# Mix order, y by token halves and v prepared ahead in the gate stage of a decoder trunk

## The reference, cut to what matters

```python
z = gelu(rms_norm(x, g_norm) @ w_in)
u, v = split(z, 2, axis=-1)
v = rms_norm(v, g_v).reshape(b, nc, CHUNK, 8, 128)
sv = einsum("gts,bnsgc->bntgc", tril(w_s), v) + b_s   # mixes the tokens of a chunk, for each of 8 groups g
y = u.reshape(b, nc, CHUNK, 8, 128) * sv
x = x + y.reshape(b, s, 1024) @ w_out
```

## Time and profile before

| what | value |
|---|---|
| median of 3 runs (lowest to highest) | 2029.73 us (2027.12 to 2032.08) |
| the profiled execution, own time | 2034.66 us |
| its span, first to last instruction | 2032.9 us |
| TensorE busy, share of the span | 96% |
| VectorE, ScalarE, GpSimd busy | 74%, 46%, 22% |
| mean granted TensorE clock | 0.98 of full speed |

### The profile page before, as it was taken

One profiled execution on the slowest core, in us unless ns is written; L12 is line 12 of the kernel. 1 busy time (PEld: TensorE's weight loads), 2 busy tenths in 40 slices (PEclk: granted clock), 3 DMA queues, 4 the chain that ended last, 5 costly groups with the idle time before them and its releaser, 6 DMA issues.

```text
span 2032.9 us, 27966 instructions
## 1 busy us (share of the span) xinstructions
PE 1947.5 (96%) x9704; PEld 1649.4 (81%) x9704; DVE 1503.0 (74%) x2202; ACT 933.9 (46%) x1620; POOL 445.5 (22%) x321
## 2 busy tenths in 40 slices
PE   7999899999999998999999799989999999989999
PEld 7988778788888886888999688867788888867887
DVE  5356658888888875786844688889887887866875
ACT  5233434544444443444412788756444444433443
POOL 0000001333333220020110445532333333310100
PEclk9999999999999998999999799999999999999999
DMA  4111142122222259680112000011222222289761
GB/s 170 43 42 42 52 155 104 62 83 83 83 82 83 83 174 311 192 207 1 42 42 69 15 11 12 22 78 68 84 83 83 83 83 83 83 240 339 142 143 63
DMA packets 62820, 198.99 MB, mean 98 GB/s; under 512 B 5008, under 2 KB 5136, under 8 KB 55568
## 3 DMA queue, kind: packets, MB, share of 16 engines
q1 hardware_dynamic: 48080, 163.29, 22.6%
q0 software_dynamic: 14656, 34.61, 7.9%
HBM read 162.22 MB, written 35.65 MB: 97 GB/s over the span
## 4 chain that ended last, share of the span: by engine, by line
PE 80%; DVE 10%; DMA 4%; ACT 3%; issue 1%; SPq 0%; POOL 0%; DVEq 0%; ACTq 0%
PE banks L2082 26%; PE banks L2084 26%; PE banks L2083 26%; DMA raw<-in_w_f_out 1%; DMA b<-c_scratch 1%; DVE t_lo L1600 1%; DMA c_scratch<-xT 1%; ACT lg L1302 1%; PE banks L2418 1%; DVE t_sum L1840 1%; DVE t_sum L1590 1%; DVE lg L1982 1%; DVE small L1989 1%; DVE fw_lo L1756 1%; DVE xT L1682 1%
## 5 line engine op out<-in xcount | busy, mean ns | idle before, releaser
L2082 PE MATMUL banks<-t_hi,fw_hi 128*128 128x512 f32 x1248 | 488.8, 392 | 11.0 <-issue 11.0
L2084 PE MATMUL banks<-t_hi,fw_lo 128*128 128x512 f32 x1248 | 486.9, 390 | 0.0
L2083 PE MATMUL banks<-t_lo,fw_hi 128*128 128x512 f32 x1216 | 474.6, 390 | 0.0
L2082 PEld LDWEIGHTS banks<-t_hi,fw_hi 128*128 128x128 f32 x1248 | 235.5, 189 | 61.3 <-issue 12.6
L2084 PEld LDWEIGHTS banks<-t_hi,fw_lo 128*128 128x128 f32 x1248 | 235.2, 188 | 49.3
L2083 PEld LDWEIGHTS banks<-t_lo,fw_hi 128*128 128x128 f32 x1216 | 229.4, 189 | 48.1 <-issue 0.5
L2082 PE MATMUL banks<-fw_hi,fw_hi 128*128 128x512 f32 x544 | 215.6, 396 | 22.4 <-DVE fw_lo L1756 22.4
L667 POOL TENSOR_TENSOR nrm<-raw 128x512 f32<-128x512 f32 x40 | 53.6, 1339 | 753.7 <-DVE fw_lo L1643 439.7
L2083 PE MATMUL banks<-fw_lo,fw_hi 128*128 128x512 f32 x544 | 214.4, 394 | 0.0
L2084 PE MATMUL banks<-fw_hi,fw_lo 128*128 128x512 f32 x544 | 214.4, 394 | 0.0
L1133 ACT ACTIVATE fw_hi<-b 128x512 fp32r<-128x512 f32 x154 | 96.9, 630 | 220.8 <-PE banks L2084 209.4
(11 more groups left out here) (196 smaller groups left out, 4208.5 us busy)
## 6 DMA issues: line engine op xcount, KB each, us to landing
raw<-in_w_f_in SPq DMA_DIRECT2D x44, 1024.0 KB, 4.9
c_scratch<-xT SPq DMA_DIRECT2D x44, 512.0 KB, 2.6
raw<-in_w_f_out SPq DMA_DIRECT2D x66, 256.0 KB, 6.6
b<-c_scratch SPq DMA_DIRECT2D x16, 1024.0 KB, 9.0
a_sum<-in_w_f_out POOLq DMA_DIRECT2D x16, 1024.0 KB, 10.4
w_raw<-in_w_ao SPq DMA_DIRECT2D x16, 512.0 KB, 3.5
x_scratch<-xT SPq DMA_DIRECT2D x4, 2048.0 KB, 7.2
xT<-x_scratch SPq DMA_DIRECT2D x8, 1024.0 KB, 9.4
```

The lines of the kernel that those rows point to most:

```text
L2082: nc.tensor.matmul(out, w_h, m_h, start=start, stop=False, **kw)
L2083: nc.tensor.matmul(out, w_h, m_l, start=False, stop=False, **kw)
L2084: return nc.tensor.matmul(out, w_l, m_h, start=False, stop=stop, **kw)
```

## The change

TensorE: mix 0 now stands between the two token halves of u tile 1, and mix 7 between those of tile 7; a new semaphore, `u_half`, tells that the first half of tile 7 is through. The other mixes stay between the tiles. The y of token half 0 is made into operands from that moment; the y of half 1 is made beside projection tiles 0 to 3. Projection tile 0 runs seven k steps before tile 1 begins. v is scaled one group further ahead (`normalised(g + 2)` behind `mixed(g)`), and the two parts of the next vn are made before mixed(g) and not after it. The diff, without the renamed semaphore and the loops' headers:

```diff
 # GpSimd: y_done starts at 1
+            pool.sem_inc(y_done, 1)
 # ScalarE
             def mixed(g):
                 act.wait_ge(mix_full, g_n.add())
+                act.wait_ge(y_done, g_n.now())
...
             def u_step(g, s):
+                act.wait_ge(mix_full, g_n.now(1))
+                vn_upper(g_n.now(2))
                 mixed(g)
-                vn_upper(g_n.now(1))
                 gate(1 - s)
...
+            act.wait_ge(mix_full, 7)
+            vn_upper(8)
             mixed(6)
-            vn_upper(8)
-            def y_upper(g):
-                act.wait_ge(y_done, g + 1)
-                nc.scalar.activation(h_hi_a[:, bass.ds(g, 1), :].rearrange("p a (n t) -> p (a n) t", t=P),
-                                     v_sb[:, :, bass.ds(g * P, P)], ACT.Copy).then_inc(y_hi_done, 1)
+            def y_upper(half, g):
+                tok, n = slice(half * HALF, (half + 1) * HALF), slice(4 * half, 4 * half + 4)
+                act.wait_ge(y_done, g + 2)
+                nc.scalar.activation(h_hi_a[:, g, tok].rearrange("p (n t) -> p n t", t=P),
+                                     v_sb[:, n, g * P:(g + 1) * P], ACT.Copy).then_inc(y_hi_done, 1)
+            act.wait_ge(u_half, 1)
+            for g in range(5):
+                y_upper(0, g)
+            mixed(7)
+            for g in (5, 6):
+                y_upper(0, g)
             act.wait_ge(tile_full[1], tiles[1].add())
-            y_upper(0)
-            y_upper(1)
             split(1)
-            mixed(7)
             act.wait_ge(u_scaled[1], tiles[1].now())
             nc.scalar.activation(ug[:, 1, :], ug[:, 1, :], ACT.Gelu).then_inc(tile_free[1], 1)
-            with act.Fori(2, KT) as g:
-                y_upper(g)
+            y_upper(0, 7)
...
+            for dt in range(KT):
+                o_square(dt // 2, dt % 2, 0)
+                split(dt % 2)
+                if dt < 4:
+                    for g in (2 * dt, 2 * dt + 1):
+                        y_upper(1, g)
 # VectorE (y_lower by halves in the same manner)
             def u_step(g, s):
+                vn_lower(g_n.now(2))
                 mixed(g, s)
-                normalised(g + 1, g_n.now(1))
+                normalised(g + 2)
                 tiles[1 - s].add()
                 scaled_u(1 - s)
                 split(1 - s)
...
+            vn_lower(8)
             mixed(6, 0)
-            normalised(7, 8)
-            tiles[1].add()
-            scaled_u(1)
-            y_lower(0)
-            y_lower(1)
-            split(1)
-            mixed(7, 1, lambda: y_lower(2))
-            with dve.Fori(3, KT) as g:
-                y_lower(g)
+            def last_tile():
+                for g in (5, 6):
+                    y_lower(0, g)
+                tiles[1].add()
+                scaled_u(1)
+                split(1)
+            for g in range(5):
+                y_lower(0, g)
+            mixed(7, 1, last_tile)    # runs it behind the bias, before the product with u
+            y_lower(0, 7)
...
+            for dt in range(KT):
+                o_add(dt // 2, dt % 2, 0)
+                split(dt % 2)
+                if dt < 4:
+                    for g in (2 * dt, 2 * dt + 1):
+                        y_lower(1, g)
 # TensorE
+            def rows_around(slot, s, between, signal=None):
+                pe.wait_ge(w_ready[slot], use[slot].add())
+                if tiles[s].some():
+                    pe.wait_ge(tile_free[s], tiles[s].now())
+                rows_half(slot, s, 0, h_hi_a, h_lo_a, signal)
+                between()
+                rows_half(slot, s, 1, h_hi_a, h_lo_a)
             rows(0, 0, h_hi_a, h_lo_a)
-            mix(0)
-            rows(1, 1, h_hi_a, h_lo_a)
+            rows_around(1, 1, lambda: mix(0))
...
-            mix(7)
+            mix(5)
+            rows(0, 0, h_hi_a, h_lo_a)
+            mix(6)
+            rows_around(1, 1, lambda: mix(7), u_half)
             pe.wait_ge(mix_free, KT)
...
-            for k in (0, 1):
+            for k in range(KT - 1):
                 pe.wait_ge(y_ready, k + 1)
                 o_step(0, 0, k)
             pe.wait_ge(w_ready[1], use[1].now())
-            for k in (0, 1):
+            for k in range(4):
                 o_step(1, 0, k)
-            for k in range(2, KT):
-                pe.wait_ge(y_ready, k + 1)
-                for s in range(2):
-                    o_step(s, 0, k)
+            pe.wait_ge(y_ready, KT)
+            o_step(0, 0, KT - 1)
+            for k in range(4, KT):
+                o_step(1, 0, k)
...
-            o_tile(0, 1)
+            o_tile(0, 1, True)    # waits for the y of half 1 at each k
```

More of the change, by code:

```diff
@@ L373, in build @@
         mix_free = sem("mix_free")
-        ug_done = sem("ug_done")
+        u_half = sem("u_half")
         y_done = sem("y_done")
@@ L979, in o_square @@
                                      .rearrange("p a t -> p (a t)"), ACT.Square).then_inc(sq_done, 1)
-            def o_body(i):
-                for s in range(2):
-                    o_square(i, s, 0)
-                    split(s)
             nc.scalar.preload_act_table(ACT.Sqrt)
-            loop(0, 4, [(use[0], 1), (use[1], 1)], o_body)
+            for dt in range(KT):
[4 more added lines that the diff above has]
+                        y_upper(1, g)
             for dt in range(KT):
@@ L1508, in _, with normalised @@
             dve.wait_ge(bs_landed, 16)
-            def normalised(g, n):
-                vf = nrm[:, 0, :].rearrange("p (n c) -> p n c", c=P)
+            vf = nrm[:, 0, :].rearrange("p (n c) -> p n c", c=P)
+            def normalised(g):
                 nc.vector.tensor_tensor(vf, v_sb[:, :, bass.ds(g * P, P)],
@@ L1515, in normalised, with vn_lower @@
                                         ALU.mult).then_inc(vf_done, 1)
+            def vn_lower(n):
                 dve.wait_ge(vn_hi_done, n)
@@ L1528, in mixed @@
                 dve.wait_ge(mix_free, g_n.now())
+                link(nc.vector.tensor_tensor(m, m, bs_bc[:, bass.ds(g, 1), :].broadcast_to([P, NCH, P]), ALU.add))
                 between()
-                link(nc.vector.tensor_tensor(m, m, bs_bc[:, bass.ds(g, 1), :].broadcast_to([P, NCH, P]), ALU.add))
                 dve.wait_ge(tile_free[s], tiles[s].now())
@@ L1543, in _ @@
             dve.wait_ge(rows_kept, 2)
-            normalised(0, 1)
+            normalised(0)
+            vn_lower(1)
             scaled_u(0)
             split(0)
+            dve.wait_ge(vn_ready, 1)
+            normalised(1)
             def u_step(g, s):
+                vn_lower(g_n.now(2))
                 mixed(g, s)
-                normalised(g + 1, g_n.now(1))
+                normalised(g + 2)
                 tiles[1 - s].add()
@@ L1558, in _, with y_lower @@
             loop(0, 3, [(use[0], 1), (use[1], 1), (g_n, 2), (steps, 2), (tiles[0], 1), (tiles[1], 1)], u_body)
+            vn_lower(8)
             mixed(6, 0)
-            normalised(7, 8)
-            tiles[1].add()
-            scaled_u(1)
[L1564 to L1569, removed]
-            y_lower(0)
-            y_lower(1)
-            split(1)
-            mixed(7, 1, lambda: y_lower(2))
-            with dve.Fori(3, KT) as g:
-                y_lower(g)
+            def y_lower(half, g):
+                tok, n = slice(half * HALF, (half + 1) * HALF), slice(4 * half, 4 * half + 4)
+                dve.wait_ge(y_hi_done, KT * half + g + 1)
+                nc.vector.tensor_tensor(h_lo_a[:, g, tok].rearrange("p (n t) -> p n t", t=P),
+                                        v_sb[:, n, g * P:(g + 1) * P],
+                                        h_hi_a[:, g, tok].rearrange("p (n t) -> p n t", t=P).bitcast(F32),
+                                        ALU.subtract).then_inc(y_ready, 1)
+            def last_tile():
[8 more added lines that the diff above has]
+            y_lower(0, 7)
             link(nc.vector.memset(acc[:, :, :], 0.0))
@@ L2127, in rows, with rows_half @@
                     pe.wait_ge(tile_free[s], tiles[s].now())
[L2128 to L2135, removed]
+                rows_half(slot, s, 0, h_hi, h_lo)
+                rows_half(slot, s, 1, h_hi, h_lo)
+            def rows_half(slot, s, half, h_hi, h_lo, signal=None):
+                tok = slice(half * HALF, (half + 1) * HALF)
+                for k in range(KT):
+                    mm = three(banks[:, 2 * s + half, :], w_hi[:, slot, k * P:(k + 1) * P],
+                               w_lo[:, slot, k * P:(k + 1) * P], h_hi[:, k, tok], h_lo[:, k, tok],
+                               k == 0, k == KT - 1)
+                if half:
+                    mm.then_inc(tile_full[s], 1)
+                    tiles[s].add()
+                elif signal is not None:
+                    mm.then_inc(signal, 1)
+            def rows_around(slot, s, between, signal=None):
[5 more added lines that the diff above has]
+                rows_half(slot, s, 1, h_hi_a, h_lo_a)
             outs = [Count() for _ in range(2)]
```

(11 more changed lines are left out.)

## The result

The changed kernel takes 2017.87 us (median of 5 runs, 2014.76 to 2019.81) against 2029.73 (5 runs, the 3 of the table above and two more, 2027.12 to 2032.08). The ratio is 0.9935, 95% interval 0.9923 to 0.9947, which is 13.2 us less, 10.8 to 15.6. The forecast was 2014.4 in a range of 2009.5 to 2020.5, faster.

The account below looks back on a forecast made before the run. TensorE, busy 1947.5 of 2032.9 us, was taken as the bound, so only its idle or low clock could pay. Gains of 5.9 + 5.7 + 2.0 + 1.7 = 15.3 us gave a median of 2014.4, range 2009.5 to 2020.5.

Parts of the forecast that it names:

- Gap A: TensorE's 3.10 us idle before mix 0; moving mix 0 inside u tile 1 was to gain 5.9 us, clock included.
- gap B: TensorE's idle between mix 7 and the output projection, 4.00 us; claimed to vanish, gaining 5.7 us, clock included.
- gap C: TensorE's idle before projection tile 2, awaiting weights; claimed 1.40 in place of 3.44 us, gaining 2.0, plus 1.7 of clock.
- The clock term: Slow clock behind the three idles, claimed regained: 1.7 in mix 0, 1.1 in tile 1, 1.5 and 1.7 in projection tiles.
- Cost zero: Preparing the next v ahead on ScalarE and VectorE: same number of instructions, claimed to cost zero, its 4.0 us chain covered.
- The prediction's other sum, 13.5: Split of y: if a half cost a whole, piece 7 would miss by about 2, gain 13.5 us, not 15.4.
- (1): Whole kernel as summed: 2014.4 us, own range 2011.5 to 2017.5, chance 0.70.
- (2): Remaining idle before projection tile 2 halves the clock or exceeds 2 us: 1.7 to 3.5 less gain, 2016 to 2018, chance 0.10.
- (3): Last y(7) or slot 1's split is late, idle returns before piece 7: gain only 9.6, 2020 us, chance 0.12.
- (4): Slower: every mix waits for the vn and gain chain of 4.0 us, costing 28 against 15.3, 2042 us, chance 0.02.
- (5): The gain is given back at a later wait that doesn't move with TensorE: 2029.7 us, chance 0.03.
- (6): No idle at all before projection tile 2: 2013 us, chance 0.03.

Follow-up runs that it names:

- before: The kernel before, unchanged, in its first profiled execution; that execution took 2034.66 us, against a median of 2029.73.
- same_again: The kernel before, unchanged, timed and profiled again; 2029.92 us beside 2030.91, ratio 0.9996.
- ahead_only: The kernel before with only v prepared ahead (loops over y and projection tiles of half 0 written out); 2031.7 us, ratio 0.9998.
- the timed filler: The kernel before with matmuls of no use filling the three idle gaps of the stage; 2029.31 us beside 2032.06, ratio 0.999.
- no_ahead: The changed kernel with v prepared as before, behind mixed(g), both mixes still inside their tiles; 2029.62 us, ratio 0.9991 to the kernel before.
- head_only: The kernel before with only mix 0 moved between the token halves of u tile 1; 2033.75 us, ratio 1.0013.
- whole_y: The changed kernel with y made whole after tile 7 and projection tiles 0 and 1 interleaved; 2026.32 us, ratio 0.9976 to the kernel before.
- after: The changed kernel in its first profile, span 2013.0 us; median 2017.87 us, ratio 0.9935 to the kernel before.
- after_again: The changed kernel, unchanged, timed and profiled again; 2016.55 us beside 2031.24 for the kernel before, ratio 0.9935.
- no_head: The changed kernel with mix 0 back between u tiles 0 and 1; 2022.49 us, ratio 0.9956 to the kernel before.
- order_2: The changed kernel with projection tile 0's last k step behind 2, not 4, steps of tile 1; 2016.22 us, ratio 0.9929 to the kernel before.

## Why the prediction was right, and where it was off

**The idle, right to a few tenths.** Gap A gone, gap B gone, gap C from 3.44 to 1.17 where I had 1.40 (the step is 1.40, of which one matmul's 0.23 is work), full clock in tile 2, steps of 12.82 in the middle: each is in the timeline after. Slacks were 2.0 and 2.1 where I had 1.1 and 1.3, because I added up instructions at their full length and in a row they overlap: five half-size ones take 3.09, not 3.45, and whole-size ones of 1.22 start 1.13 to 1.21 apart. Tile 3's weights, priced as tight, came 0.9 early, and no tenths were lost.

**The clock term, mis-sized as an average.** The sum took 6.0 us of slow clock (1.7, 1.1, 1.5, 1.7) out of one execution, and took it off the median, though this execution stood 4.9 us over the median. Three profiles with all three gaps of the kernel before have S = 135.64, 132.49 and 132.10 (before, same_again, ahead_only), mean 133.4; the changed kernel has 120.21 twice. The gain in S is thus 15.4, 12.3 and 11.9, on average 13.2. That both ratios say 13.2 as well is in part luck, with three draws. At clock 1.00 S is 130.80, so the low clock costs 2.6 on average by these three and 1.7 by the timed filler, not 6.0. That puts the forecast of 2014.4 some 2 us too fast (medians 2017.87 and 2016.55), though 15.3 lies within the intervals of both timings, so that the times alone don't refute it.

**"Cost zero" of preparing v ahead, right as a cost and wrong as a reading.** My chain of 4.0 us against 5.45 and 10.9 was for the new order. I didn't work out what the old order would need, 8.9 us after a mix where the new one needs 2.8, and so didn't see that both moved mixes hang on this part. no_ahead shows it for both and head_only for mix 1: without it the gaps come back in front of mix 1 and mix 7 and the whole change is worth 0 to 3.5 us. The total came out right because the change has both parts.

**The split of y.** Its 16 instructions are busy for 10.2 us on VectorE against 9.4 for the 8 whole ones; the rule of the Trainium skill against many small tiles (VectorE: DVE Perf Modes, "The TRN2 errata") holds in direction, with under 1 us, and all of it lies beside TensorE. In return whole_y, which gives up the halves and the step order together, is 9.0 to 9.8 us slower. The prediction's other sum, 13.5 if a half cost a whole, counted five halves only; with seven in front of piece 7, and its own two, the same working makes it some 3.4 late, not 2 (an estimate). No half cost that much.

**Rivals.** The first median, 2017.87, lies just outside the own range of (1), 2011.5 to 2017.5, and inside that of (2); the second, 2016.55, lies in both. So the time doesn't choose between them, the traces do. (2), a low clock behind the rest of gap C: not drawn in after, after_again, no_head or no_ahead, all with a step of 1.40. (3), a late last chain: no. (4), the chain as a wait in every step: no, the middle steps are 12.82 as before. (5), given back later: no sign. From projection tile 3 to the end of the span it is 1784.6 and 1785.1 us in the two profiles of the changed kernel, and 1787.5, 1786.2 and 1787.3 in before, same_again and ahead_only. (6), no gap C: not in this kernel, but one number away (order_2).

## What to carry to other kernels

A gap in front of a small step isn't closed by moving the step: work out how long after its predecessor the step's operands are ready, for the old order of the feeding engines too; the reordering that seems to cost and gain nothing may be what the others hang on. Low clock behind an idle has to be taken from several traces. Idle itself repeated to hundredths in this stage, so one trace was enough there; it doesn't everywhere (the 1.57 at 1814.21 in the earlier trace rows is 1.15 in same_again). Where two projection tiles share a feed, finish one of them early enough for the chain of its next weights.

## What the runs showed of the hardware

The same idle of 2.95 us in front of the same matmul was followed by half clock for all of mix 0 in one execution and by none in another (window 122.20:131.00, clock 1.00). Low clock can also hide a wait: with it gone, 0.5 us for y_lower came to light. And executions of one kernel, whose idle in this stage two profiles show alike to 0.01, spread over 8 us (2027.04 to 2034.84 in 23 runs).
